# Weight sums of gate and up: made by GpSimd in its own order instead of by VectorE

## The reference

```
def swiglu(x, w_gate, w_up, w_down):
    return (jax.nn.silu(x @ w_gate) * (x @ w_up)) @ w_down
...
f1 = swiglu(rms_norm(x, ffn1_pre_g[l]), ffn1_w_gate[l], ffn1_w_up[l], ffn1_w_down[l])
x = x + FFN_RESIDUAL_WEIGHT * rms_norm(f1, ffn1_post_g[l])
```

## Time and profile before

| | |
|---|---|
| median of 3 runs | 3876.63 us |
| profiled execution, its own time | 3875.97 us |
| its span | 3874.2 us |
| mean granted TensorE clock | 0.985 of full |
| TensorE busy | 3732.6 us, 96% |
| VectorE busy | 2370.9 us, 61% |
| ScalarE busy | 1653.9 us, 43% |
| GpSimd busy | 1691.9 us, 44% |

### The profile page before, as it was taken

The page is one execution under the profiler, slowest core; times in us unless marked ns, Lnnn a source line. Parts: engine busy times, 40 slices in busy tenths (PEclk is TensorE's granted clock), DMA queues, the critical chain, the costliest instruction groups (busy, mean ns, idle before and its releaser), DMA issues.

```text
span 3874.2 us, 50420 instructions
## 1 busy us (share of the span) xinstructions
PE 3732.6 (96%) x19892; PEld 3038.4 (78%) x19892; DVE 2370.9 (61%) x3104; ACT 1653.9 (43%) x2799; POOL 1691.9 (44%) x1112
## 2 busy tenths in 40 slices
PE   7999999999999898999999899999999999999998
PEld 5888887666655466888888799999878988888877
DVE  7767784643555548667684766644577156666663
ACT  5333344422222235333444454411572256666663
POOL 4555554244444544555553244422532233443464
PEclk9999999999999899999999999999999999999999
DMA  3234574200000122234574011221121310000014
GB/s 110 96 107 154 167 263 152 88 23 22 22 22 17 44 79 69 95 106 152 186 249 138 29 43 44 66 91 63 45 72 53 136 32 23 30 25 28 30 67 140
DMA packets 143405, 327.30 MB, mean 84 GB/s; under 512 B 16896, under 2 KB 20512, under 8 KB 142784
## 3 DMA queue, kind: packets, MB, share of 16 engines
q1 hardware_dynamic: 131280, 279.70, 21.9%
q0 software_dynamic: 9328, 41.75, 2.9%
q10 hardware_dynamic: 2560, 2.61, 0.2%
HBM read 252.37 MB, written 71.63 MB: 84 GB/s over the span
## 4 chain that ended last, share of the span: by engine, by line
PE 78%; DVE 12%; ACT 4%; POOL 3%; issue 2%; DMA 1%; SPq 0%; ACTq 0%; DVEq 0%; POOLq 0%
PE ps L955 6%; PE ps L956 6%; PE ps L957 6%; PE ps L415 5%; PE ps L416 5%; PE ps L417 5%; PE ps L4260 4%; PE ps L975 3%; PE ps L973 3%; PE ps L974 3%; PE ps L4192 2%; PE ps L4194 2%; PE ps L4193 2%; PE ps L2003 2%; PE ps L4244 2%; PE ps L2005 2%
## 5 line engine op out<-in xcount | busy, mean ns | idle before, releaser
L389 POOL TENSOR_TENSOR wlo<-raw,whi 128x1024 fp32r<-128x1024 f32 x154 | 376.3, 2448 | 483.8 <-ACT whi L380 483.7
L415 PE MATMUL ps<-xh,whi 128*128 128x352 f32 (+1 forms) x1400 | 473.9, 338 | 7.0 <-DVE xl L672 2.7
L416 PE MATMUL ps<-xh,wlo 128*128 128x352 f32 (+1 forms) x1400 | 451.3, 322 | 0.0
L417 PE MATMUL ps<-xl,whi 128*128 128x352 f32 (+1 forms) x1400 | 450.7, 322 | 0.0
L862 POOL TENSOR_TENSOR fwl<-fpb,fwh 128x512 fp32r<-128x512 f32 x204 | 301.9, 1490 | 277.4 <-ACT fwh L852 277.2
L862 POOL TENSOR_TENSOR fwl<-fpa,fwh 128x512 fp32r<-128x512 f32 x202 | 291.0, 1450 | 279.5 <-ACT fwh L852 279.5
L4565 POOL TENSOR_TENSOR ospl<-osp,osph 128x672 fp32r<-128x672 f32 (+4 forms) x144 | 191.1, 1327 | 358.9 <-ACT osph L4386 357.7
L415 PEld LDWEIGHTS ps<-xh,whi 128*128 128x128 f32 x1400 | 265.8, 190 | 18.8 <-POOL wlo L389 6.3
L416 PEld LDWEIGHTS ps<-xh,wlo 128*128 128x128 f32 x1400 | 264.9, 189 | 7.9 <-issue 2.1
L417 PEld LDWEIGHTS ps<-xl,whi 128*128 128x128 f32 x1400 | 264.9, 189 | 0.0
L955 PE MATMUL ps<-fxh,fwh 128*128 128x512 f32 x640 | 249.2, 389 | 0.0
(11 more groups left out here) (506 smaller groups left out, 9700.6 us busy)
## 6 DMA issues: line engine op xcount, KB each, us to landing
raw<-in_w_dram SPq DMA_DIRECT2D x154, 512.0 KB, 3.7
hs_scratch<-u SPq DMA_DIRECT2D x176, 256.0 KB, 2.4
u<-hs_scratch SPq DMA_DIRECT2D x118, 256.0 KB, 2.9
fpa<-in_fg_dram SPq DMA_DIRECT2D x88, 256.0 KB, 3.7
fpb<-in_fg_dram SPq DMA_DIRECT2D x88, 256.0 KB, 3.8
fpa<-in_fd_dram SPq DMA_DIRECT2D x88, 256.0 KB, 3.3
fpb<-in_fd_dram SPq DMA_DIRECT2D x88, 256.0 KB, 4.0
acc<-hs_scratch SPq DMA_DIRECT2D x80, 256.0 KB, 2.9
```

Of the source, the lines that this page charges most:

```text
L389: pool.x.tensor_tensor(K.wlo[n % 3][:, :], K.raw[n % 2][:, :], K.whi[n % 3][:, :], ALU.subtract).then_inc(*S.up("w_lo", n))
L415: pe.x.matmul(out, wh, xh, start=k == 0, stop=False)
L416: pe.x.matmul(out, wl, xh, start=False, stop=False)
L417: last = pe.x.matmul(out, wh, xl, start=False, stop=k == K - 1)
```

## The change

The raw sums of gate and up leave VectorE's stream and go into GpSimd's, between its low halves; the semaphore that ScalarE waits for is pool_fsum instead of dve_fsum. The down stage keeps dve_fsum. In the main loop GpSimd makes, in iteration n, the low half of step n+4 and then the raw sum of step n+5.

```
-        e.wait_ge("dve_fsum", (f, same(step, "M6")))
+        e.wait_ge("pool_fsum", (f, same(step, "M6")))
...
     e.x.tensor_tensor(raw_tile(K, step, d), raw_tile(K, step, a), raw_tile(K, step, b),
-                      op).then_inc(*S.up("dve_fsum", (f, n)))
+                      op).then_inc(*S.up("pool_fsum", (f, n)))
...
-        act.wait_ge("dve_fsum", (f, n))
+        act.wait_ge("dve_fsum" if down else "pool_fsum", (f, n))
...
     dve_mix(dve, f, "M7", "sum", pre)
-    raw_sum(dve, f, 9)
     std(1, 0)
     late_done(dve, norms)
     dve_mix(dve, f, "M7", "lo", pre)
-    raw_sum(dve, f, 10)
-    raw_sum(dve, f, 11)
     std(1, 1)
-    raw_sum(dve, f, 12)
...
-        if n + 5 < FIRST_DOWN:
-            raw_sum(dve, f, n + 5)
...
     pool_mix(pool, f, "M5")
-    for n in range(4, 10):
+    for n in range(4, 9):
         pool_operand(pool, f, n)
+    raw_sum(pool, f, 9)
+    pool_operand(pool, f, 9)
+    raw_sum(pool, f, 10)
     pool_mix(pool, f, "M4")
     for n in range(10, 12):
+        raw_sum(pool, f, n + 1)
         pool_operand(pool, f, n)
     for n in range(FIRST_GATE, NSTEP):
         pool_operand(pool, f, n + 4)
+        if n + 5 < FIRST_DOWN:
+            raw_sum(pool, f, n + 5)
```

More of the change, by code:

```diff
@@ L803, in raw_sum @@
         e.wait_ge("fw_lo", (f, same(step, "M1")))
-        e.wait_ge("dve_fsum", (f, same(step, "M6")))
+        e.wait_ge("pool_fsum", (f, same(step, "M6")))
     elif m == "M7":
         e.wait_ge("fw_lo", (f, same(step, "M6")))
-        e.wait_ge("dve_fsum", (f, same(step, "M3")))
+        e.wait_ge("pool_fsum", (f, same(step, "M3")))
     e.x.tensor_tensor(raw_tile(K, step, d), raw_tile(K, step, a), raw_tile(K, step, b),
-                      op).then_inc(*S.up("dve_fsum", (f, n)))
+                      op).then_inc(*S.up("pool_fsum", (f, n)))
 def dve_down_sum(dve, f, n):
```

## The result

The changed kernel takes 3890.39 us, the median of 6 runs (3888.34 to 3891.04); the kernel before takes 3878.67 on the same chips (6 runs, 3873.36 to 3880.04). The ratio is 1.0032, with a 95% interval of 1.0022 to 1.0042. The forecast was slower by 12.2 us, to 3888.5; measured are 11.7, to 3890.4. The interval runs from 8.5 to 16.3 us, so the medians alone don't tell 11.7 from a few us more or less.

What follows compares the result with a forecast made beforehand. TensorE bounds the stage, busy for all of it except the hole at 80 to 100 us. Terms 2.4 + 0.8 + 2.9 = 6.1 us a block, 12.2 for two, gave 3888.5 us; range 3879 to 3908.

Steps and rivals of the forecast that it cites:

- The entry: Tile 2's hole: five paid VectorE turns delay the sum of step 12, TensorE restarts later; +2.4 us a block.
- After the restart: Just after tile 2's hole: sum 16 comes about 3 us later against TensorE, stalling it once; +0.8 us a block.
- Early tiles: Tiles before 11: the loop of GpSimd and ScalarE takes 18.4 us, under TensorE's 19.04; nothing lost.
- Late tiles: Sums of tiles 13 to 21: loop 19.3 us against TensorE's 19.04, late copy of M1; +2.9 us a block.
- A: Rival, chance 0.24: only the entries lose, the loop stays under 19.04 us in late tiles too; 5.6 us, 3882.
- B: Rival, chance 0.15: a turn costs GpSimd 0.69 us, not 0.48, or more operations meet; 15.3 us a block, 3907.
- C: Rival, chance 0.06: faster, the chain at the entry gets shorter; gain of 0.3 us a block, 3876.
- does nothing: Case that the change doesn't do what it says, the sums not being on GpSimd; given no chance.

Runs made afterwards that it cites:

- The kernel with two turns fewer: The changed kernel with T2 and T4 of tiles 11 to 20 reading their second source from a PSUM bank; ratio to before 1.0005.
- the kernel with tiles 3 to 11: The kernel before with only the sums of tiles 3 to 11 moved to GpSimd, the others left on VectorE; ratio to before 0.9999.

## Why the prediction was right

**What bounds the kernel** was read rightly. TensorE is at 100% up to 290 us in both, and no sum taken from VectorE gave anything. That the copy of M1 ends the hole, and not the low half or "issue" that the views name, is shown by the two kernels in which it moved and the hole with it.

**The entry**: forecast +2.4, measured 12.71 - 10.06 = 2.65 for the hole and 2.9 of stage time with tile 2's sums alone. The counted chain holds: sum 12 ended at 91.29, 22.25 us after the start of the first low half (69.04), and the forecast was 22.0. Inside it two small errors cancel. A sixth turn, of the operations that follow the silu of std(1,1), lengthens the sum of step 12 (1.72) and was not in the count, which had VectorE parked to the end. And a place with the port free is 1.22 where I took 1.25.

**After the restart**: forecast +0.8, found 0 in block 1 and about 0.6 in block 2 (a wait of 0.37 at 1572.92 and a first matmul at a slower pace). This term was mis-sized. In block 1 TensorE ran at the lower clock from 95.5 to 101.3 us (granted 0.51, the 1.2 GHz level), through all of M6 and into M3, 13 matmuls at 0.43 where it was 8 before; in block 2 it was 8, where it was 13 before. That gives GpSimd time to catch up, and costs about 1.0 itself (5 x 0.20). The block with 13 had no stall in tile 3 and the one with 8 had one. The kernel with two turns fewer, whose sums are those of the change there, shows the same: 11 slow matmuls and no stall in block 1, 7 and the wait of 0.37 in block 2. No run sets the number of slow matmuls, so it stays an argument from four blocks. Both blocks then add up: 2.65 + 1.0 + 5.4 (below) = 9.05 in block 1, against 9.0 of stage time, and 1.22 (the hole) - 1.0 + 0.6 + 5.0 = 5.8 in block 2, against 5.7. I had no term for the clock.

**Early tiles**: forecast 0, found 0, by the kernel with tiles 3 to 11.

**Late tiles**: forecast +2.9 a block, found 5.4 of stage time in block 1 and 5.0 in block 2. The mechanism was right in its place (the copy of M1, M6), its onset (by hand in the second late tile, tile 14; eight stalls from tile 14 on) and its cause (T2 and T4 out, stalls out). The size was off: 19.3 a tile was forecast and 19.67 to 19.69 measured. I had counted four and a half turns; the rows show T4, h1, s0, h0 and T2 paid in full (0.40 to 0.46 each) and half of s1 (about 0.23), so five and a half. s1 stays half outside the hand-over, where I had let it slide in, and h1 is paid as a whole and not by half.

**The sum** was 12.2 and the medians say 11.7, but the two blocks' stages say 14.7 in the profiled execution. Part of the agreement is luck: in block 1 the late tiles were put 2.5 too low, the restart 0.8 too high and the slow matmuls (1.0) at nothing; in block 2 the clock gave back 1.0 and shortened the hole by 1.4, of which the forecast knew nothing.

**The rivals.** A (entries only) is out by the kernel with the sums of tiles 3 to 21, 1.0018. It was near: two turns fewer and the late tiles are 19.04. B (a turn costs GpSimd VectorE's whole 0.69) is out: the groups of three low halves are 4.23 with T2's turn and 3.80 without, 0.43 apart. Moving one source of T2 and T4 to PSUM took their turns away. The Trainium skill's rule for the shared port (SBUF — State Buffer, Who interferes with whom: a VectorE operation contends with a GpSimd one that reads SBUF when both its inputs are in SBUF, and not when at most one is) holds here in its kind; for the size the rows decide. C and "does nothing" are out.

## What to carry to other kernels

An engine with idle time is not free for more work if each piece is one link in a chain of engines: count the loop (operations, hand-overs, and the other engine's turns at a shared port) against the period of the engine that bounds, here 17.1 + 2.6 against 19.04. Where a wait ends is often an instruction that the view doesn't name; look for what ended 0.1 us before, and for what it stood behind in its engine's queue. A wait that is removed from an in-order stream can come back at the next thing that stream makes late: of six reorderings of the entry all shortened the first hole, and only two, both of the kernel before, kept 0.2% of the time or more. And before a difference of 1 to 3 us in one stage is explained, count the slow matmuls in it and ahead of it.

## What the runs showed of the hardware that was not expected

After each long hole of the two stages (4.04 to 12.77 us) TensorE ran for a while at the lower clock, matmuls 0.43 us apart and not 0.23 (granted 0.51 from 95.5 to 101.3 us, the 1.2 GHz level). How many were slow doesn't follow the hole: 8 and 13 in the two blocks before (holes of 10.06 and 10.07), 13 and 8 after (12.71 and 11.29).

The wait of 2.9 us ahead of block 2's stage shows it best, as the instructions around it are the same in all thirteen kernels. In the profiled executions it was followed by no slow matmul in seven kernels (the kernel before among them), by 6 or 7 in five (the change among them) and by 14 in one. After a wait of 0.70 us there was none. A second wait in the same entry brought the lower clock a second time in block 1 (2.09, 3.22 and 3.79 us), so a hole cut in two can pay for slow matmuls twice; second waits of 1.99 and 2.23 us in block 2 did not.

VectorE's operations with a PSUM source never waited for GpSimd (0.67 to 0.69 in every row of the two stages), with GpSimd busy for 83% of the stage.
